# Five convolution banks as one ring, reorder blocks waited for singly, loads and first steps moved, soft plus in three steps

## The reference, cut to what matters

```
proj = rmsnorm(x) @ w_in
x1, x2, v, q, k   = three-tap convolution along the tokens of proj's first columns
A  z  = x1 * long_conv(v, kspec[0]);  y_hy = x2 * long_conv(z, kspec[1])      512 channels
B  y_ml = sigmoid(o) * norm(mLSTM forward + mLSTM backward)                    4 heads x 128
x  = x + concat(y_hy, y_ml) @ w_out
x  = x + (silu(gate) * val) @ w_down,  val, gate = three-tap convolution of rmsnorm(x) @ w_up
```

## Time and profile before

| | |
|---|---|
| median of 3 runs | 2383.06 us (2382.06 to 2390.59) |
| the profiled execution | 2382.36 us, span 2380.5 us |
| busy: PE, PEld | 2253.8 us (95%), 1862.0 us (78%) |
| busy: DVE, ACT, POOL | 1188.4 us (50%), 785.5 us (33%), 146.4 us (6%) |
| mean granted clock of TensorE | 0.983 |

### The profile page before, as it was taken

How to read it: one execution, slowest core, us unless ns; L and a number is a source line. 1 busy time by engine, 2 the same in 40 slices (tenths; PEclk the granted TensorE clock), 3 DMA queues, 4 the chain that set the end, 5 groups by cost and what they waited for, 6 DMA issues and landing times.

```text
span 2380.5 us, 26125 instructions
## 1 busy us (share of the span) xinstructions
PE 2253.8 (95%) x10340; PEld 1862.0 (78%) x10340; DVE 1188.4 (50%) x1655; ACT 785.5 (33%) x1193; POOL 146.4 (6%) x163
## 2 busy tenths in 40 slices
PE   6999999998998979877899999999999999999998
PEld 5788888887886867666788888888888887888886
DVE  6676777645732766657365333343333334324332
ACT  5432333344434434544244212122122123324221
POOL 0221131100111000100000000000000000000000
PEclk8999999999998989999999999999999999999999
DMA  4354544444556566765644111121112112545542
GB/s 143 111 151 131 143 142 129 142 155 159 176 181 205 154 188 180 220 162 159 224 139 169 54 61 51 53 80 62 53 49 69 55 53 102 177 115 171 156 150 85
DMA packets 213588, 307.23 MB, mean 129 GB/s; under 512 B 15480, under 2 KB 143864, under 8 KB 213466
## 3 DMA queue, kind: packets, MB, share of 16 engines
q1 hardware_dynamic: 200858, 256.00, 35.3%
q0 software_dynamic: 11312, 46.14, 5.3%
q10 hardware_dynamic: 1296, 3.41, 0.4%
HBM read 207.38 MB, written 72.16 MB: 117 GB/s over the span
## 4 chain that ended last, share of the span: by engine, by line
PE 51%; DVE 0%; ACT 0%; issue 0%; DVEq 0%; POOL 0%
PE mlp_acc L128 10%; PE mlp_acc L130 10%; PE mlp_acc L129 10%; PE mlp_dacc L128 7%; PE mlp_dacc L130 7%; PE mlp_dacc L129 7%; PE mlp_acc L2596 0%; DVE out_s_lo L2494 0%; DVE up_u L245 0%; ACT up_u L2437 0%; DVE mlp_h_lo L2516 0%; DVE out_w_lo L2489 0%; DVE down_d_lo L2538 0%; ACT out_s_hi L2412 0%; DVE up_u L249 0%
## 5 line engine op out<-in xcount | busy, mean ns | idle before, releaser
L128 PE MATMUL mlp_acc<-mlp_h_hi,up_w_hi 128*128 128x512 f32 x1056 | 411.6, 390 | 0.2 <-DVE mlp_h_lo L2516 0.2
L129 PE MATMUL mlp_acc<-mlp_h_lo,up_w_hi 128*128 128x512 f32 x1056 | 411.4, 390 | 0.0
L130 PE MATMUL mlp_acc<-mlp_h_hi,up_w_lo 128*128 128x512 f32 x1056 | 411.3, 390 | 0.0
L2521 DVE TENSOR_TENSOR up_w_lo<-up_w_raw,up_w_hi 128x1024 fp32r<-128x1024 f32 x44 | 53.8, 1225 | 388.3 <-ACT up_w_hi L2429 388.3
L128 PEld LDWEIGHTS mlp_acc<-mlp_h_hi,up_w_hi 128*128 128x128 f32 x1056 | 198.4, 188 | 41.4 <-DVE mlp_h_lo L2516 0.6
L130 PEld LDWEIGHTS mlp_acc<-mlp_h_hi,up_w_lo 128*128 128x128 f32 x1056 | 198.4, 188 | 41.1
L129 PEld LDWEIGHTS mlp_acc<-mlp_h_lo,up_w_hi 128*128 128x128 f32 x1056 | 198.4, 188 | 40.9
L128 PE MATMUL mlp_dacc<-down_d_hi,down_s_hi 128*128 128x512 f32 x528 | 206.4, 391 | 5.3 <-DVE down_d_lo L2538 5.3
L129 PE MATMUL mlp_dacc<-down_d_lo,down_s_hi 128*128 128x512 f32 x528 | 206.2, 391 | 0.0
L130 PE MATMUL mlp_dacc<-down_d_hi,down_s_lo 128*128 128x512 f32 x528 | 206.2, 390 | 0.0
L2429 ACT ACTIVATE up_w_hi<-up_w_raw 128x1024 fp32r<-128x1024 f32 x44 | 46.6, 1060 | 460.2 <-PE mlp_acc L130 460.2
(11 more groups left out here) (243 smaller groups left out, 3894.1 us busy)
## 6 DMA issues: line engine op xcount, KB each, us to landing
in_w_raw<-arg_w_in_t SPq DMA_DIRECT2D x58, 512.0 KB, 3.7
down_s_raw<-g_scratch SPq DMA_DIRECT2D x48, 512.0 KB, 4.6
up_w_raw<-arg_w_up_t SPq DMA_DIRECT2D x44, 512.0 KB, 3.5
g_scratch<-up_prod POOLq DMA_DIRECT2D x22, 768.0 KB, 3.5
filt_tab<-arg_fwd SPq DMA_DIRECT2D x32, 512.0 KB, 3.8
mix_classes<-mix_split SPq DMA_DIRECT2D x48, 256.0 KB, 8.6
mix_kf<-k_scratch SPq DMA_DIRECT2D x48, 256.0 KB, 2.8
mix_split<-mix_classes SPq DMA_DIRECT2D x48, 256.0 KB, 5.0
```

The lines of the kernel that those rows point to most:

```text
L128: pe.matmul(out, w_hi, x_hi, start=first, stop=False)
L129: pe.matmul(out, w_hi, x_lo, start=False, stop=False)
L130: return pe.matmul(out, w_lo, x_hi, start=False, stop=last)
L2521: dve.tensor_tensor(w_lo[i % 2][:, :, :], raw[i % 2][:, :, :], w_hi[i % 2][:, :, :].bitcast(F32), ALU.subtract).then_inc(sem["w_low"], 1)
```

## The change

Six edits:
1. The five convolution banks (`xacc` x2, `gacc`, `vyacc` x2) become one ring of five, `vyacc` 0 to 4, taken in turn by split, join, turn, inverse and forward; each use waits for the reader of the fifth use before it.
2. `to_split` becomes one semaphore per block: a join waits for its own block. Two waits are new: SP waits for all blocks of a stream ahead of the first reorder of its second convolution, and ACT ahead of the first turned copy.
3. The first `gap` of head steps, behind the leading splits, is 3.2 in place of 6. This also shifts all head steps behind it against the convolution steps.
4. The first `load` that has a `back` within the next 12 steps is put behind it.
5. Soft plus is three steps for the planner in place of one; the order on ACT may have other steps between them.
6. The planner's delay for the gates' load is 9 in place of 4.

```diff
         if kind == "load_gates":
-            return "SP", 1.0, 4.0, [("store", i) for i in gate_tiles] + [("drain_k",)]
+            return "SP", 1.0, 9.0, [("store", i) for i in gate_tiles] + [("drain_k",)]
         if kind == "softplus":
-            return "ACT", 7.5, 0, [("load_gates",)]
+            return "ACT", 2.8, 0, [("softplus", a[0] - 1) if a[0] else ("load_gates",)]
         if kind == "forget":
-            return "DVE", 3.0, 0, [("softplus",)]
+            return "DVE", 3.0, 0, [("softplus", 2)]
...
-    conv.append(("gap", 6))
+    conv.append(("gap", 3.2))
...
     schedule += [(x[0],) + x[2:] for x in heads[at:]]
+    for n, step in enumerate(schedule):
+        if step[0] == "load":
+            near = [m for m in range(n, min(n + 12, len(schedule))) if schedule[m][0] == "back"]
+            if near:
+                schedule.insert(near[-1], schedule.pop(n))
+                break
...
         if kind == "split":
             v_at[args] = len(v_at)
-            before[args] = vy[-2] if len(vy) >= 2 else None
+            before[args] = vy[-5] if len(vy) >= 5 else None
             vy.append(("v_copied", len(v_at)))
...
+        elif kind == "inverse":
+            before["inverse", args] = vy[-5] if len(vy) >= 5 else None
+            vy.append(("g_copied", args[0] + 1))
+        elif kind == "forward":
+            before["forward", args] = vy[-5] if len(vy) >= 5 else None
+            vy.append(("multiplied", args[0] + 1))
...
-    vy_of = {step: n % 2 for n, step in enumerate(x for x in schedule if x[0] in ("split", "join", "turn"))}
+    vy_of = {step: n % 5 for n, step in enumerate(x for x in schedule if x[0] in ("split", "join", "turn", "inverse", "forward"))}
...
-        xacc = [p.ps(f"xacc{b}", [P, 2, HC]) for b in range(2)]
-        gacc = p.ps("gacc", [P, 2, HC])
-        vyacc = [p.ps(f"vyacc{b}", [P, 2, HC]) for b in range(2)]
+        vyacc = [p.ps(f"vyacc{b}", [P, 2, HC]) for b in range(5)]
...
                 def shuffle_classes(o, st, b):
                     sp.wait_ge(sem["v_copied"], v_at[o, st, b] + 1)
+                    if (o, b) == (1, 0):
+                        for back in to_split[st]:
+                            sp.wait_ge(back, 16)
...
-                    if g >= 2:
-                        pe.wait_ge(sem["multiplied"], g - 1)
+                    free(before["forward", (g,)])
...
                     pe.wait_ge(sem["multiplied"], g + 1)
-                    if g:
-                        pe.wait_ge(sem["g_copied"], g)
+                    free(before["inverse", (g,)])
...
-                    if b == 0:
-                        pe.wait_ge(to_split[st], 16 * nts[s] * (o + 1))
+                    pe.wait_ge(to_split[st][b], 16 * (o + 1))
                     free(before["join", (o, st, b)])
...
                 def copy_turned(st, b):
                     act.wait_ge(sem["transposed"], t_at[st, b] + 1)
+                    if b == 0:
+                        for back in to_split[st]:
+                            act.wait_ge(back, 16 * ORDER)
```

More of the change, by code:

```diff
@@ L1123, in root_of, with softplus @@
                     act.activation(root[:, :], cbank[:, 0, 0:HC], ACT.Sqrt, scale=0.5 * n * n).then_inc(sem["rooted"], 1)
[L1125 to L1131 removed]
+                def softplus(n):
+                    if n == 0:
+                        act.wait_ge(sem["gates_loaded"], 32)
+                        act.activation(ab[:, :], gf[:, :], ACT.Abs).then_inc(sem["g_act"], 1)
+                    elif n == 1:
+                        act.wait_ge(sem["g_act"], 1)
+                        act.activation(ab[:, :], ab[:, :], ACT.Exp, scale=-1.0).then_inc(sem["g_act"], 1)
+                    else:
+                        act.wait_ge(sem["g_act"], 2)
+                        act.activation(ab[:, :], ab[:, :], ACT.Ln, bias=1.0).then_inc(sem["soft"], 1)
                 def exponential(j):
@@ L1536, in long_convolutions_and_heads @@
             y_at[args] = len(y_at)
-            before["join", args] = vy[-2] if len(vy) >= 2 else None
+            before["join", args] = vy[-5] if len(vy) >= 5 else None
             vy.append(("z_ready", len(y_at)))
@@ L1540, in long_convolutions_and_heads @@
             t_at[args] = len(t_at)
-            before["turn", args] = vy[-2] if len(vy) >= 2 else None
+            before["turn", args] = vy[-5] if len(vy) >= 5 else None
             vy.append(("copied", len(t_at)))
+        elif kind == "inverse":
[4 more added lines that the diff above has]
+            vy.append(("multiplied", args[0] + 1))
         elif kind == "keys":
@@ L1609, in long_convolutions_and_heads @@
         z_loaded, y_stored, tab_loaded, head_stored = ahead.z_loaded, ahead.y_stored, ahead.tab_loaded, ahead.head_stored
-        to_classes, to_split = ([p.sem(f"{x}{st}") for st in range(len(streams))] for x in ("to_classes", "to_split"))
+        to_classes = [p.sem(f"to_classes{st}") for st in range(len(streams))]
+        to_split = [[p.sem(f"to_split{st}_{b}") for b in blocks(st)] for st in range(len(streams))]
         k_loaded = [p.sem(f"k_loaded{b}") for b in range(ring)]
@@ L1806, in forward @@
                         pe.wait_ge(to_classes[st], 16 * nts[s] * (o + 1))
-                    if g >= 2:
-                        pe.wait_ge(sem["multiplied"], g - 1)
+                    free(before["forward", (g,)])
+                    out = vyacc[vy_of["forward", g]]
                     for u in range(2):
-                        last = pe.matmul(xacc[g % 2][:, u, :], tab[s][:, t, u, 0, :], classes(st)[:, 2 * t + u, :], start=True, stop=True)
+                        last = pe.matmul(out[:, u, :], tab[s][:, t, u, 0, :], classes(st)[:, 2 * t + u, :], start=True, stop=True)
                     last.then_inc(sem["x_ready"], 1)
@@ L1816, in inverse @@
                     pe.wait_ge(sem["multiplied"], g + 1)
-                    if g:
-                        pe.wait_ge(sem["g_copied"], g)
+                    free(before["inverse", (g,)])
+                    out = vyacc[vy_of["inverse", g]]
                     for u in range(2):
                         for i in range(2):
-                            last = pe.matmul(gacc[:, u, :], tab[s][:, t, u, 1 + i, :], prod[g % 2][:, u, i, :],
+                            last = pe.matmul(out[:, u, :], tab[s][:, t, u, 1 + i, :], prod[g % 2][:, u, i, :],
                                              start=i == 0, stop=i == 1)
@@ L1905, in copy_classes @@
                     act.wait_ge(sem["g_ready"], g + 1)
-                    act.activation(classes(st)[:, 2 * t:2 * t + 2, :], gacc[:, :, :], ACT.Copy).then_inc(sem["g_copied"], 1)
+                    act.activation(classes(st)[:, 2 * t:2 * t + 2, :], vyacc[vy_of["inverse", g]][:, :, :], ACT.Copy).then_inc(sem["g_copied"], 1)
                 def turned(st):
@@ L1980, in multiply @@
                         dve.wait_ge(sem["g_ready"], g - 1)
-                    x, kk = xacc[g % 2], kf[g % ring]
+                    x, kk = vyacc[vy_of["forward", g]], kf[g % ring]
                     dve.tensor_tensor(prod[g % 2][:, :, 0, :], x[:, :, :], kk[:, :, :], ALU.mult)
```

11 lines of the change are left out of this document (2 added, 9 removed).

## The result

The changed kernel took 2352.89 us (median of 4, 2350.22 to 2354.04), the kernel before beside it 2386.14 us: a ratio of 0.9859, 95% interval 0.9840 to 0.9878, so 33.6 us faster (29 to 38). The profiled execution took 2350.22 us (span 2348.4), 32.1 us less than the one before. The forecast was 2339 (2328 to 2347 for the likeliest case), its range 2326 to 2358. It started from 2383.06 us for the kernel before, which took 3.1 us more beside the changed one.

What follows compares the result with a forecast made beforehand. PE was taken as nearly always busy, losing time to waits on DMAs, DVE and ACT and slow clock behind them. Terms A to F sum to -50.0 us, DVE takes back 6: 2339 us as a median, range 2326 to 2358.

Steps and rivals of the forecast that it cites:

- likeliest case: Whole kernel: the forecast itself, 2328 to 2347 us, given a chance of 0.62.
- A: Projections: soft plus in three steps removes a 7.88 us stall and slow clock; -9.1 us (bounds -7 and -9.7).
- B: First forward transform: PE stands until its last reorder block lands, small waits go; +1 us (bounds -1 and +4).
- C: Join 0 2 0: reorder blocks issued ahead of load 3 remove its wait and slow clock; -11.5 us (bounds -5 and -14).
- counter-term of 2.6 us: Within C: a filter load now queues behind the blocks, and 2.6 us of DVE's wait for it stays visible.
- D: Joins 0 1 0 and 1 1 0 wait only for their first block; -10.4 us (bounds -6 and -10.4).
- sign of being wrong: Forward 16, 32 or 40: PE waiting over 3 us for mix_classes would show the forecast wrong.
- E: Splits, joins, turns, inverses: five banks in a ring remove waits for bank readers; -13.0 us (bounds -6 and -14).
- the ring gives nothing: Rival at the joins: they wait because DVE has other work, not for few banks; 2351 us, chance 0.09.
- F: Head steps: a transform or join in front removes waits of turned heads and attends; -7 us (bounds -3 and -8).
- The 6 us that DVE takes back: Multiplies on DVE: it is late next as PE comes earlier, so 6 us of the summed gain is lost.
- transfers take back half: Rival at the forward transforms: reorders wait on queue pace, so PE stands there instead; 2352 us, chance 0.17.

Runs made afterwards that it cites:

- F undone: The changed kernel with the first gap of head steps at 6 in place of 3.2: 2363.6 us, 0.9893 of the kernel before.
- the other start: The changed kernel with SP issuing head 1's five loads and the first two gate loads later, behind filter loads: 2341.87 us, 0.9815 of the kernel before.
- DVE's steps moved: The kernel with the other start, with DVE's weighting steps of three heads put behind multiplies that PE waits for: 2346.34 us, 0.9827 of the kernel before.

## Why the prediction was right, and where its terms were off

The direction and the range held; the time was 14 us too low, outside the 2328 to 2347 us of the likeliest case, and inside the range where that had been stretched over two rivals. 3 of the 14 us are the kernel before, which took 2386.14 in place of 2383.06 us; in gain it was 44 us forecast and 33.6 measured. By terms:

- **A, soft plus** (-9.1): right. 8.45 us by the start of the stage, 9.3 us alone.
- **B, gap at the start** (+1): near; +1.9 up to inverse 3. The stall was foreseen at about 10 us and is 10.76. It was called the price of the smaller gap; the last runs show that most of it is removable, since another order of SP's first issues took 6 us off this stretch.
- **C, back 0 2 ahead of load 3** (-11.5): its stretch gives -11.46, and the waits of join 0 2 0 are gone. The ring has some part in this stretch too (it is 3.3 us shorter with the ring alone); the run with gap and load loop alone gives -10.1 there. The counter-term of 2.6 us, "a filter load now queues behind the blocks", has the right size and the wrong cause: the wait of split 1 2 0 stays when load 3 is moved. DVE is busy there.
- **D, blocks singly** (-10.4): mis-sized. Alone it measured 2.1 us (at most 4.3), on the ring 0 to 5. The failed step is the one that took the wait and its slow clock as gone once the first block has landed; what comes next in that place, the two banks and the weighting on DVE, is the 7.9 us of the earlier trace rows growing to 16.4, while PE stood 10.0 us less for DMAs. With the ring the later splits meet the queue at forward 40, for which it named 3 us as a sign of being wrong: 3.60.
- **E, ring** (-13.0): right in size, 10.7 us alone, 12 us taken out of the changed kernel, and the waits that it named are gone. But it was added up from waits and 1.5 us of slow clock, and in the trace of the ring alone nearly half of the stage's gain (7.7 of 16.9 us) is busy time of PE. Its stretches at 1.2 GHz are 6.8 us shorter, which is at most 3.4 of the 7.7; the rest no term foresaw, and its cause is open. So a part of the fit is luck. The rival "the ring gives nothing" is refuted, though its 2351 us is within 2 us of the measured time. The Trainium skill, in "TensorE: Matmul & The Clock Gate", section "HAM oscillation — how this bites in real kernels", tells of a kernel where a second PSUM buffer gave no further gain; here more banks gave 10.7 us, so this kernel disagrees.
- **F, heads between transforms** (-7): failed. The waits for `mix_og`, which were to fall under 1.5 us, are 5.6 where they were 5.2, "issue" 5.7 where it was 5.8, and those of turned heads for `mix_e` rose from 1.0 to 4.0, of which 3.0 are there with F undone as well. With two banks the new head order even costs: 5.7 us from split 1 2 3 on, in the run of the gap alone. Of the kernel before, beside the 3.6 of the earlier trace rows:

```profile
PE mix_bank_b L1890 <- DVE mix_og L2084: 1.6, 2, 0.9
PE mix_bank_b L1890 <- DVE mix_e L2005: 1.0, 2, 0.8
...
PE mix_vyacc L1840 <- DVE mix_z L1992: 0.8, 2, 0.4
```

  The step that counted a wait as removed because another PE step was put in front of it looked at PE's order only. All engines walk one list, so the step was put in front on DVE too; that this is why the waits stayed is argued from the order, not tried.
- **The 6 us that DVE takes back**: about what shows in new waits for DVE (splits 4.0, turns 1.6 more than before, turned heads 3.0 more), less the waits for `mix_prod`, which fell from 5.6 to 1.7 instead of growing: 4.7 us, without any slow clock behind them. Near in size, other place.

A, B, C and E, with the 6 us taken off, make 26.6 of the 33.6 us, and D and F were to bring 17.4; 7.0 us are left for them. The four parts alone sum to 26.9 us (9.3, 4.8, 10.7, 2.1), 6.7 less than the whole. Each of these numbers has a margin of 2 to 4 us and the whole one of 4 to 5, so together about 7 us: that the parts are worth more together is not shown. Two parts were measured both ways: the ring gives 10.7 us alone and 12 in the changed kernel, the blocks 2.1 and 0 to 5.

The rival "transfers take back half" had a true part: the queue holds forward 0 and forward 40, 14.4 us in all. Its 2352 us is the nearest to the measured time, but by other terms than it named: it had C at 4 and E at 8 us, which gave 10 to 11 and 11 to 12, and it had 5 us each for D and the head steps, which gave 5 together at most. Nothing in the change makes the queue faster.

## What to carry to other kernels

When a wait is removed, ask what the same engine needs next, in the order of the engine that serves it: here the first block landed in time, and PE then stood for a bank that DVE frees behind 3.5 us of other work, so that an edit forecast at 10.4 us gave 2.1. A step put in front of a waiting one helps only if the engine that is waited for doesn't also have to do it first. Read a stall on a transfer as a question of what stands ahead in the queue: with loads that nothing needed yet issued later, the stage's first 46 us became 40. And when a part gives less alone than forecast, compare the stretches before calling it useless: the gap's own stretch gave its 10 us, and others took most of them back.

## What the runs showed of the hardware that was not expected

How late the same issues land varies between executions. Forward 40 waited 3.60 and 2.81 us in two executions of the changed kernel, 0.40 us with the other start and 5.76 us with DVE's steps moved, although SP's order from load 7 on is the same in all. In the last of these the final two reorders needed up to 13.1 us to land, and with the start alone 9.0:

```profile
L1679 SPq DMA_DIRECT2D mix_classes<-mix_split x2: 598/604/610, 1024.8 to 1025.5; - x2
...
DMA to landing us min/median/max: 8.8/11.0/13.1
```

```profile
L1672 SPq DMA_DIRECT2D mix_classes<-mix_split x2: 532/532/532, 1025.9 to 1027.4; - x2
...
DMA to landing us min/median/max: 8.1/8.6/9.0
```

In the slower case the eight landings come 1.2 to 1.8 us apart but for two gaps of 4.9 us (1025.80 to 1030.68, 1033.66 to 1038.57); in the faster case they come 0.7 to 1.3 us apart but for one gap of 4.8 us (1028.71 to 1033.55). A gate load issued among them lands in the faster case ahead of the last three (1032.13) and in the slower case between the last two (1036.06). Between load 7 and forward 40 the 16 DMA engines are busy nearly all the time in both (shares 0.94 and 0.97), with 225 and 259 GB/s. What makes these gaps was not tried and stays open; they may be a part of the 2 to 12 us by which executions of one kernel differed.
